# Last down projection, residual and last norm laid out by tokens, in a two-block fp32 transformer kernel

## Chip, core and metric

One NeuronCore of a Trainium2 chip runs the whole program once. The metric is the device time of one execution in microseconds. The core's engines are TensorE (PE in the profile), VectorE (DVE), ScalarE (ACT), GpSimd (POOL) and SyncE (SP, which here only issues DMAs); they run their own instruction streams side by side and meet through semaphores.

## What is computed

256 tokens of width 2048 pass through two blocks, all in fp32. The first block is a hybrid mixer (a state-space part and a gated short convolution), cross attention to a memory and a SwiGLU MLP; the second is an attention layer with three kinds of heads and a gated MLP with a short convolution on its gate. What the change touches is the end:

```python
    # second block; x is [256 tokens, 2048]
    x = x + einsum('bse,ed->bsd', y, w_o)                       # residual after attention
    h = rmsnorm_2(x, ffn_norm)
    g = causal_dwconv_2(h @ w_gate, conv_w, conv_b)
    u = h @ w_up                                                # width 5632
    x = x + (silu(g) * u) @ w_down                              # last down projection
    return rmsnorm_2(x, final_norm)                             # x * rsqrt(mean(x^2) + 1e-6) * final_norm
```

## The kernel before

**Layout.** Activations stand with features on the 128 partitions and tokens along the free axis: the residual `X` is 16 tiles of 128 features x 256 tokens. Every fp32 operand is split into two fp32r numbers, high and low: the weights into `whi` and `wlo`, the activations into the two halves of the buffers `H` and `Y`. A product is high x high + high x low + low x high.

**Weight stream.** All weights come in one fixed order as 930 subs of eight 128x128 blocks (512 KB each). SP loads a sub into one of four `raw` buffers; ACT copies it to `whi` (`split`, L830), DVE subtracts to give `wlo` (`split`, L1227); `whi` and `wlo` are rings of five (`NW`). ACT may only split sub s once PE has finished sub s - 5 (`sub_done`).

**Products.** `gemm_tiles()` lists the tiles in order; `tensor_program` walks them. In the usual form a block of weights is the stationary operand: one matmul of 512 columns (`whi` with the pair of activation halves) and one of 256 (`wlo` with the high half). In the narrow form (`NARROW`, among them `ao2`) it is three of 256. In the wide form (`WIDE`: `wv`, `va`, `vb`, `vc`) the activations of 128 tokens are stationary and `whi` or `wlo` of up to four blocks move: three matmuls for each k and each half t of the tokens, the result lies by tokens. The second MLP's down projection has three parts, `d10`, `d11`, `d12`, of 256, 256 and 192 blocks, in the usual form, eight tiles each. Two accumulators of two PSUM banks alternate between tiles; four further banks serve side work.

**Order.** The stream is cut into slots of four blocks. In the slot where a block count is reached each engine's program runs `side.step(t)` (norms, attention tasks, transposes, each a generator that goes one step per slot), then on odd slots `split(t // 2 + 5)`, then `leave` (takes a finished tile out of its accumulator, on DVE in the tile's last slot plus `GATHER_LAG`, on ACT plus `LAG`) and on DVE `follow` (three slots later). Each engine does this strictly in its own order. So in DVE's program the residual addition of an `ao2` or `d` tile (`leave`, L1675 and L1677) stands behind the split of the same slot. PE runs `side.step` after the last matmul of a slot.

**End.** The last norm (`norm` with n = 6) is summed over features: ACT squares each pair of tiles, POOL adds seven of the eight squares, PE multiplies the sums by a matrix of ones, partly in the stream (before `d12`'s last tile is through), partly after it. Then DVE and ACT make the root with a Newton refinement on 128x256. ACT multiplied each tile by `final_norm_2` before; DVE multiplies six pairs by the root (L1210), POOL two (L1779), and SP and ACT store each pair as it is ready (L471, L1199).

Of the kernel before, what the change touches and what calls it, by code (L numbers as in the profile page):

```python
# [13 lines left out]
P = 128  # L14
# [16 lines left out]
    ("conv_w_2", 132), ("conv_b_2", 44), ("final_norm_2", 16), ("dt_bias", 1), ("a_log", 32),  # L31
# [32 lines left out]
WIDE = ("wv", "va", "vb", "vc")  # L64
NARROW = ("bc", "dt", "xs", "xo", "ao2")

HELD = ("wq", "g0", "qa", "g1", "d00", "d01", "d02", "d10", "d11", "d12")
# [10 lines left out]
def gemm_tiles():  # L78
# [13 lines left out]
    for f in range(2):  # L92
# [6 lines left out]
        for part, (a0, a1) in enumerate(PARTS):  # L99
            for j in range(a0 // 2, a1 // 2):  # L100
                out += [(f"g{f}", j, "H", 0, 16, 2), (f"u{f}", j, "H", 0, 16, 2)]
            out += [(f"d{f}{part}", j, "Y", 0, a1 - a0, 2) for j in range(8)]
# [58 lines left out]
NORM = {"x": 0, "wo2": 1, "xo": 2, "d02": 3, "mid": 4, "ao2": 5, "d12": 6}  # L161
RESIDUAL = ("wo1", "wo2", "xo", "d00", "d01", "d02", "ao1", "ao2", "d10", "d11", "d12")
# [3 lines left out]
def tasks():  # L166
# [21 lines left out]
    out += [(first_slot("g1") + 5, "norm", 5), (N_SLOT - 3, "norm", 6)]  # L188
# [5 lines left out]
LAG = {"bc": 4, "xs": 5, "z": 3, "g0": 1, "g1": 1, "wo2": 2, "xo": 2, "d02": 2, "ao2": 2}  # L194
# [15 lines left out]
for _t, _kind, _i in TASKS:  # L210
# [15 lines left out]
    "xs": [("b", 6, 8, "xs_copy", 1, 1)],  # L226
    "ssd": [("b0", 0, 2, "ssd_exp", 2, 1), ("b1", 0, 2, "ssd_exp", 2, 2), ("o", 6, 9, "ssd_z", 1, 1)],
# [72 lines left out]
def idle(n):  # L300
# [5 lines left out]
    "pe_own act_own dve_own pool_own raw0 raw1 raw2 raw3 x0 x1 x2 x3 x4 x5 x6 x7 c1 raw_first whi_first wlo_first scaled vec mem c2 rel rows hank out "  # L306
# [9 lines left out]
    "bnd_s bnd_max bnd_exp bnd_w bnd_turn bnd_copy bnd_pv bnd_sq bnd_n bnd_root bnd_y gain_x pool_x"  # L316
# [3 lines left out]
class Chip:  # L320


    def __init__(self, nc, ctx, d, out):
# [50 lines left out]
        self.HK = AR[:, 3072:5120]  # L374
        self.rows = nc.dram_tensor("rel_rows", [8, 512], F32).ap()
# [16 lines left out]
    def xt(self, k, n=1):  # L392
        return self.X[:, k * T:(k + n) * T]

# [44 lines left out]
def sync_program(e, c):  # L439
# [29 lines left out]
    for i in range(6):  # L469
        s.wait_ge("gain_x", i + 1)  # L470
        e.dma_start(c.out[:, 2 * i * T:(2 * i + 2) * T], c.xt(2 * i, 2)).then_inc(c.sems["out"], 16)  # L471
    s.wait_ge("out", 128)
# [4 lines left out]
def tensor_program(e, c):  # L477
# [19 lines left out]
    def norm(n):  # L497
# [3 lines left out]
        p.wait_ge("sum_add", 7 * n + (6 if n == 6 else 7))  # L501
        if n < 6:
            last = mm(bank, c.ones, c.SUM, True, True)
        else:
            mm(bank[:, 0:T], c.ones, c.SUM[:, 0:T], True, False)
            mm(bank[:, 0:T], c.ones, c.SUM[:, T:2 * T], False, False)
            yield from idle(3)
            p.wait_ge("sq", 8 * n + 8)
            mm(bank[:, 0:T], c.ones, c.SQ[1][:, 0:T], False, False)
            last = mm(bank[:, 0:T], c.ones, c.SQ[1][:, T:2 * T], False, True)  # L510
        p.then_inc(last, "norm_sum")
# [232 lines left out]

    def done(stage, j):

        b, n = bank_of(stage, j)
        return f"acc{b}", n + 1

    side = Side({"norm": norm, "mnorm": mnorm, "mcol": mcol, "rcol": rcol, "sc": sc, "cb": cb, "dt": dt, "xs": xs, "ssd": ssd,  # L750
                 "grp": grp, "xa": xa, "dfa": dfa, "dfb": dfb, "stk": stk, "bnd": bnd})
# [19 lines left out]
    for stage, j, op, k0, K, m in GEMM:  # L771
# [3 lines left out]
        if stage in WIDE:  # L775
            for k in range(k0, k0 + K):
                wh, wl = halves(b, m)
                for t in range(2):
                    out, start = c.acc[n][:, t, 0:m * P], k == k0
                    xh, xl = c.hi(op, k)[:, t * P:(t + 1) * P], c.lo(op, k)[:, t * P:(t + 1) * P]  # L780
                    mm(out, xh, wh, start, False)
                    mm(out, xl, wh, False, False)
                    last = mm(out, xh, wl, False, k == k0 + K - 1)
                b = finish(b, m, last)
# [14 lines left out]
    for t in range(N_SLOT, N_SLOT + 4):  # L799
        side.step(t)  # L800
# [1115 lines left out]
```

## Time and profile before

| | |
|---|---|
| median of 3 runs | 2743.03 us (2742.43 to 2743.47) |
| the profiled execution | 2743.26 us, of which the span of instructions is 2741.3 us |
| PE busy | 2717.2 us, 99% |
| DVE busy | 1949.9 us, 71% |
| ACT busy | 1284.8 us, 47% |
| POOL busy | 94.7 us, 3% |
| DMA | 499 MB, mean 182 GB/s |
| granted TensorE clock | 0.998 of 2.4 GHz |

All times in the views are microseconds from the start of the span. A matmul is recorded from its start to its modelled end, and matmuls overlap in the array, so what a matmul costs the stream is the distance from its start to the next one's start, not its recorded length.

### The profile page before, as it was taken

The page shows a single profiled execution, that of the slowest core. Times are in us where ns is not written, and L with a number is a line of the kernel's source. Part 1 is how long each engine was busy: PE and PEld are TensorE (multiplying, and loading weights), DVE is VectorE, ACT ScalarE, POOL GpSimd, SP SyncE. Part 2 cuts the span into 40 slices and gives each one's busy share as a digit, 9 for nine tenths or more (in the row PEclk, how much of TensorE's full clock was granted, in tenths as well). Part 3 has the DMA queues.
Part 4 walks back from the last instruction along what each step waited for, and adds up shares of the span by engine and source line. Part 5 has one row for each costly group of instructions (what it writes and reads, how often), then busy time and mean ns, then how long its engine had stood idle before and what let it go on. Part 6 is the DMA issues. An engine that isn't in the chain of part 4 may idle for free.

```text
span 2741.3 us, 39113 instructions
## 1 busy us (share of the span) xinstructions
PE 2717.2 (99%) x16174; PEld 2378.5 (87%) x16174; DVE 1949.9 (71%) x2378; ACT 1284.8 (47%) x1634; POOL 94.7 (3%) x69
## 2 busy tenths in 40 slices
PE   8999999999999999999999999999999999999998
PEld 7888999888898888888888888888988888888886
DVE  7777777876768665666566886776777757775775
ACT  5444455754545443344344554545544433443444
POOL 1000000011101000000000110000100000000001
PEclk9999999999999999999999999999999999999999
DMA  6555555446555555555555555454455555555553
GB/s 240 191 185 185 175 164 173 145 160 223 182 169 189 187 191 194 191 190 189 190 185 193 191 183 170 150 168 144 164 183 185 200 190 178 193 199 190 187 192 124
DMA packets 138192, 499.07 MB, mean 182 GB/s; under 512 B 15248, under 2 KB 16280, under 8 KB 137888
## 3 DMA queue, kind: packets, MB, share of 16 engines
q1 hardware_dynamic: 136224, 491.67, 54.2%
q10 hardware_dynamic: 1792, 4.91, 0.5%
q8 instruction: 127, 2.08, 0.3%
q14 instruction: 49, 0.40, 0.0%
HBM read 494.41 MB, written 2.11 MB: 181 GB/s over the span
## 4 chain that ended last, share of the span: by engine, by line
PE 98%; DVE 1%; DMA 1%; ACT 0%; POOL 0%; issue 0%; DVEq 0%; ACTq 0%; POOLq 0%
PE PS L481 97%; DMA raw<-in_w_in 0%; DVE wlo L1227 0%; POOL AR L1738 0%; ACT whi L830 0%; DMA XG<-in_x 0%; DVE XG L1677 0%; DVE XG L1210 0%; PE PS L573 0%; DVE H L1221 0%; PE PS L727 0%; PE PS L649 0%; ACT AR L837 0%; PE PS L616 0%; DVEq L1785 0%
## 5 line engine op out<-in xcount | busy, mean ns | idle before, releaser
L481 PE MATMUL PS<-H,whi 128*128 128x512 f32 (+1 forms) x5472 | 1788.9, 381 | 8.7 <-DVE wlo L1705 7.9
L1227 DVE TENSOR_TENSOR wlo<-raw,whi 128x1024 fp32r<-128x1024 f32 x929 | 1127.7, 1231 | 638.5 <-ACT whi L830 634.5
L481 PE MATMUL PS<-H,wlo 128*128 128x256 f32 x5072 | 1412.6, 278 | 0.0
L830 ACT ACTIVATE whi<-raw 128x1024 fp32r<-128x1024 f32 x929 | 969.5, 1057 | 921.2 <-PE PS L481 883.2
L481 PEld LDWEIGHTS PS<-H,whi 128*128 128x128 f32 x5472 | 1001.8, 188 | 220.7 <-issue 8.8
L481 PEld LDWEIGHTS PS<-H,wlo 128*128 128x128 f32 x5072 | 956.3, 189 | 3.5 <-issue 3.1
L481 PE MATMUL PS<-Y,whi 128*128 128x512 f32 (+1 forms) x2240 | 719.0, 376 | 1.1 <-DVE XG L1677 0.8
L481 PE MATMUL PS<-Y,wlo 128*128 128x256 f32 x2048 | 569.3, 278 | 0.0
L481 PEld LDWEIGHTS PS<-Y,whi 128*128 128x128 f32 x2240 | 407.8, 188 | 84.0 <-DVE XG L1677 2.0
L481 PEld LDWEIGHTS PS<-Y,wlo 128*128 128x128 f32 x2048 | 385.6, 188 | 0.5 <-issue 0.2
L1549 DVE TENSOR_REDUCE AR<-PS 128x512 f32<-128x1024 f32 x140 | 171.6, 1225 | 14.6
L1738 POOL TENSOR_TENSOR AR<-AR 128x512 f32<-128x512 f32 x48 | 70.5, 1470 | 2003.8 <-ACT AR L837 2002.8
L815 ACT ACTIVATE AR<-AR 128x512 f32<-128x512 f32 x64 | 40.5, 633 | 211.8 <-DVE AR L1237 138.4
L481 PE MATMUL PS<-whi,H 128*128 128x512 f32 (+1 forms) x384 | 105.0, 361 | 0.0
L1210 DVE TENSOR_TENSOR AR<-AR 128x512 f32<-128x512 f32 x114 | 78.9, 692 | 34.7 <-ACT AR L815 32.3
L481 PE MATMUL PS<-AR 128*128 128x256 f32 (+8 forms) x580 | 99.4, 354 | 2.8 <-ACT AR L837 2.2
L1144 ACT ACTIVATE Y<-AR 128x512 fp32r<-128x512 f32 x44 | 27.8, 632 | 150.0 <-DVE AR L1666 150.0
L1237 DVE SCALAR_TENSOR_TENSOR AR<-AR 128x255 f32<-128x255 f32 (+2 forms) x192 | 92.9, 484 | 6.8
L481 PEld LDWEIGHTS PS<-AR 128*128 128x128 f32 (+3 forms) x580 | 61.5, 170 | 22.4 <-issue 11.6
L481 PEld LDWEIGHTS PS<-whi,H 128*128 128x128 f32 x384 | 67.0, 189 | 10.3 <-issue 1.0
L1219 DVE TENSOR_TENSOR Y<-AR,Y 128x512 fp32r<-128x512 f32 (+1 forms) x68 | 42.7, 628 | 37.4 <-ACT Y L1144 34.5
L481 PE MATMUL PS<-wlo,H 128*128 128x512 f32 (+1 forms) x192 | 68.2, 355 | 0.0
(173 smaller groups left out, 895.6 us busy)
## 6 DMA issues: line engine op xcount, KB each, us to landing
raw<-in_ffn SPq DMA_DIRECT2D x528, 512.0 KB, 4.1
raw<-in_w_in SPq DMA_DIRECT2D x177, 512.0 KB, 4.5
raw<-in_w_qkv SPq DMA_DIRECT2D x96, 512.0 KB, 3.7
raw<-in_w_out SPq DMA_DIRECT2D x64, 512.0 KB, 4.2
raw<-in_w_o SPq DMA_DIRECT2D x40, 512.0 KB, 3.6
raw<-in_w_q SPq DMA_DIRECT2D x8, 512.0 KB, 3.9
raw<-in_w_k SPq DMA_DIRECT2D x8, 512.0 KB, 4.3
raw<-in_w_v SPq DMA_DIRECT2D x8, 512.0 KB, 4.6
```

The source lines that it names most:

```text
L481: return e.matmul(out, l, r, start=start, stop=stop)
L815: return e.activation(dst, src, ACT.Silu)
L830: a.then_inc(e.activation(c.whi[:, s % NW, :], c.raw[:, s % NRAW, :], ACT.Copy), "whi")
L1144: a.then_inc(e.activation(c.hi("Y", 2 * (j - 8 * part), 2), two(q), ACT.Copy), "y_hi")
L1210: return e.tensor_tensor(two(dst), two(src), both(r), ALU.mult)
L1219: v.then_inc(e.tensor_tensor(c.lo(op, k, n), src, hi, ALU.subtract), made_)
L1227: v.then_inc(e.tensor_tensor(c.wlo[:, s % NW, :], c.raw[:, s % NRAW, :], c.whi[:, s % NW, :].bitcast(F32), ALU.subtract), "wlo")
L1237: v.then_inc(e.scalar_tensor_tensor(dst[:, sh:T], src[:, 0:T - sh], taps(width - 1 - sh), dst[:, sh:T], ALU.mult, ALU.add), name if sh == ...
L1549: v.then_inc(e.tensor_reduce(two(dst), c.acc[b].rearrange("p m (h t) -> p m t h", h=2), AX, ALU.add), f"acc{b}", turn + 1)
L1738: g.then_inc(e.tensor_tensor(c.SUM, c.SUM, c.SQ[i % 2], ALU.add), "sum_add")
```

## The change

The down projection of the second MLP, parts `d10`, `d11` and `d12`, goes over to the wide form: four tiles of four blocks' width in each part, with the weights as moving operand and the result by tokens. The residual is turned for it: eight side tasks `xt`, one for each `ao2` tile, transpose two tiles of `X` on PE (four transposes of 128x128) in the second slot after the tile's end, once DVE's residual addition of that tile is done; ACT copies the bank to `XT`. The last norm's gain is loaded as a 1 MB tensor repeated over the partitions. `XT` is [128 tokens, 2 halves, 2048]; DVE adds each accumulator of 128x1024 to it.

In `d12` the last tile is walked in two orders: for its first four k both token halves together, for its last eight first half 0 and then half 1. A semaphore `half` marks half 0's last matmul. The norm is now a sum along the free axis: ACT's square with an accumulated sum for each piece of 512 features and each half. For pieces 0 to 2 the squares are made in the stream, and DVE multiplies them by the gain. At the end each half runs its own chain: addition, square, sum, mean, root, Newton on one column; then DVE finishes pieces 3 and 2, which SP stores, and ACT pieces 0 and 1, which it stores as 512 KB in one. POOL no longer takes part in the last norm, and PE no longer has the norm's matmuls. The host lays the weights out in the new order and reads the output by tokens.

```diff
-WIDE = ("wv", "va", "vb", "vc")
+WIDE = ("wv", "va", "vb", "vc", "d10", "d11", "d12")
-HELD = ("wq", "g0", "qa", "g1", "d00", "d01", "d02", "d10", "d11", "d12")
+HELD = ("wq", "g0", "qa", "g1", "d00", "d01", "d02")
+LAST = ("d12", 3)
...
-            out += [(f"d{f}{part}", j, "Y", 0, a1 - a0, 2) for j in range(8)]
+            out += [(f"d{f}{part}", j, "Y", 0, a1 - a0, 4 if f else 2) for j in range(4 if f else 8)]
...
+    out += [(END[NUM["ao2", j]] // 4 + 1, "xt", j) for j in range(8)]
-    out += [(first_slot("g1") + 5, "norm", 5), (N_SLOT - 3, "norm", 6)]
+    out += [(first_slot("g1") + 5, "norm", 5)]
...
@@ sync_program
-    for i in range(6):
-        s.wait_ge("gain_x", i + 1)
-        e.dma_start(c.out[:, 2 * i * T:(2 * i + 2) * T], c.xt(2 * i, 2)).then_inc(c.sems["out"], 16)
+    for t in range(2):
+        for n, j in enumerate((3, 2)):
+            s.wait_ge("gain_x", 2 * t + n + 1)
+            e.dma_start(c.out[:, c.tok(t, j)], c.XT[:, c.tok(t, j)]).then_inc(c.sems["out"], 16)
@@ tensor_program
+    def xt(j):
+        bank = take("xt", j, "b")
+        p.wait_ge(*done("ao2", j))
+        for t in range(2):
+            for i in range(2):
+                last = e.transpose(bank[:, t * T + i * P:t * T + (i + 1) * P], c.xt(2 * j + i)[:, t * P:(t + 1) * P], c.ident)
+        p.then_inc(last, "xt_turn")
+        yield
...
         if stage in WIDE:
...
+            begin, both_halves = b, K - 8 if (stage, j) == LAST else K
+            order = [(k, t) for k in range(both_halves) for t in range(2)]
+            order += [(k, t) for t in range(2) for k in range(both_halves, K)]
+            for k, t in order:
+                if version:
+                    p.wait_ge("y_made", made(version, k))
+                wh, wl = halves(begin + k * m, m)
+                out, start = c.acc[n][:, t, 0:m * P], k == 0
+                xh, xl = c.hi(op, k)[:, t * P:(t + 1) * P], c.lo(op, k)[:, t * P:(t + 1) * P]
+                mm(out, xh, wh, start, False)
+                mm(out, xl, wh, False, False)
+                last = mm(out, xh, wl, False, k == K - 1)
+                if t:
+                    b = finish(begin + k * m, m, last)
+                elif (stage, j) == LAST and k == K - 1:
+                    p.then_inc(last, "half")
@@ scalar_program
+    def xt(j):
+        if j == 0:
+            a.wait_ge("y_made", made("ao", 15))
+            e.dma_start(c.fgain, c.d["fgain"]).then_inc(c.sems["fgain"], 16)
+        yield
+        a.wait_ge("xt_turn", j + 1)
+        dst = c.XT.rearrange("p (t n) -> p t n", t=2)[:, :, j * T:(j + 1) * T]
+        a.then_inc(e.activation(dst, c.bank("xt", j, "b").rearrange("p (t n) -> p t n", t=2), ACT.Copy), "xt_copy")
+        yield
...
+        if stage == "d12" and j < 3:
+            a.wait_ge(*done(stage, j))
+            for t in range(2):
+                final_square(j, t)
+            load(LN_EXP)
...
+    for t in range(2):
+        a.wait_ge("last_x", t + 1)
+        final_square(3, t)
+        r = c.fst[:, 10 + t:11 + t]
+        refine(r, c.fst[:, 8 + t:9 + t], "fin_mean", t + 1, "fin_root")
+        a.wait_ge("fin_gain", 6)
+        a.wait_ge("fin_ok", t + 1)
+        for j in range(2):
+            a.then_inc(e.activation(c.XT[:, c.tok(t, j)], c.XT[:, c.tok(t, j)], ACT.Copy, scale=r))
+        a.wait_ge(*a.at)
+        e.dma_start(c.out[:, c.tok(t, 0, 2)], c.XT[:, c.tok(t, 0, 2)]).then_inc(c.sems["out"], 16)
@@ vector_program, leave and follow
+        if stage in ("d10", "d11", "d12"):
+            b, turn = bank_of(stage, j)
+            x = c.XT.rearrange("p (t n) -> p t n", t=2)[:, :, j * 512:(j + 1) * 512]
+            v.wait_ge("xt_copy", 2 * j + 2)
+            v.wait_ge("sub_done", subs(stage, j))
+            v.wait_ge(*v.at)
+            v.then_inc(e.tensor_tensor(x, x, c.acc[b], ALU.add), f"acc{b}", turn + 1)
...
+        if stage == "d12" and j < 3:
+            v.wait_ge("fgain", 16)
+            v.wait_ge("fsq", 2 * j + 2)
+            for t in range(2):
+                x = c.XT[:, c.tok(t, j)]
+                v.then_inc(e.tensor_tensor(x, x, c.fgain[:, j * 512:(j + 1) * 512], ALU.mult), "fin_gain")
@@ vector_program, end
+    b, _ = bank_of(*LAST)
+    for t in range(2):
+        x2, x3 = c.XT[:, c.tok(t, 2)], c.XT[:, c.tok(t, 3)]
+        m, r, u = (c.fst[:, i + t:i + t + 1] for i in (8, 10, 12))
+        if t:
+            v.wait_ge("sub_done", N_SUB)
+        else:
+            v.wait_ge("half", 1)
+        v.wait_ge(*v.at)
+        v.then_inc(e.tensor_tensor(x3, x3, c.acc[b][:, t, :], ALU.add), "last_x")
+        v.wait_ge("fsq", 7 + t)
+        v.then_inc(e.tensor_reduce(m, c.fst[:, 4 * t:4 * t + 4], AX, ALU.add))
+        v.wait_ge(*v.at)
+        v.then_inc(e.tensor_scalar(m, m, 1.0 / 2048, c.col("eps6"), ALU.mult, ALU.add), "fin_mean")
+        newton(r, m, u, "fin_root", t + 1, "fin_ok")
+        v.wait_ge(*v.at)
+        v.then_inc(e.scalar_tensor_tensor(x3, x3, r, c.fgain[:, 1536:2048], ALU.mult, ALU.mult), "gain_x")
+        v.then_inc(e.tensor_scalar(x2, x2, r, None, ALU.mult), "gain_x")
```

## Rows read from the trace of the kernel before

**Rows 1.** The page's part 1: busy time, share of the span, instructions.
```profile
PE 2717.2 (99%) x16174; PEld 2378.5 (87%) x16174; DVE 1949.9 (71%) x2378; ACT 1284.8 (47%) x1634; POOL 94.7 (3%) x69
```
**Rows 2.** The waits of PE: total, times, longest; four shorter lines follow.
```profile
PE PS L481 <- DVE wlo L1705: 7.9, 1, 7.9
```
**Rows 3.** The chain that ended last, at its end: start, length, what.
```profile
2725.46 0.72 PE PS L481 x4
...
2726.21 0.70 DVE XG L1675
...
2727.65 0.64 ACT AR L837
...
2732.61 0.69 DVE XG L1210
2733.30 1.67 DVEq L1785
```
**Rows 4.** Stores: 40 slices of 0.425 us from 2725; engines' busy and DMA.
```profile
GB/s 0 0 0 0 0 0 0 0 0 0 0 0 0 0 0 0 0 0 0 0 0 140 386 92 260 386 381 207 294 390 371 381 390 386 381 386 106 0 0 0
...
2736.90:2740.40 3.50, 0.00 (x0) 0.00 (x0) 1.54 (x3) 0.00 (x0) 0.00 (x0) 0.50 1.00 372
```
**Rows 5.** Stretches d10, va, vb, ao2: length, PE busy (count), clock, DMA, GB/s.
```profile
2170.42:2259.17 88.75, 88.75 (x514) 1.00 0.61 201
...
1619.50:1663.55 44.05, 44.05 (x198) 1.00 0.60 198
...
1745.52:1773.97 28.45, 28.45 (x140) 1.00 0.43 140
1945.84:1991.90 46.06, 46.06 (x386) 1.00 0.56 183
```
**Rows 6.** Timeline of PE in va, first and last of 12 groups: start, length.
```profile
1639.76 0.62 PE L481 MATMUL PS<-whi,H 128*128 128x512 f32 x2
...
1647.92 0.39 PE L481 MATMUL PS<-whi,H 128*128 128x512 f32 x1
```
**Rows 7.** Timeline of ACT and DVE around an ao2 tile's end.
```profile
1957.61 1.06 ACT L830 ACTIVATE whi<-raw 128x1024 fp32r<-128x1024 f32 x1 [0.50 <-PE PS L481]
1958.71 1.23 DVE L1227 TENSOR_TENSOR wlo<-raw,whi 128x1024 fp32r<-128x1024 f32 x1 [0.86 <-ACT whi L830]
1960.04 0.69 DVE L1677 TENSOR_TENSOR XG<-XG,PS 128x512 f32<-128x512 f32 x1
```
**Rows 8.** Timeline of PE around a group of four transposes, stage xs.
```profile
387.18 0.40 PE L481 MATMUL PS<-H,whi 128*128 128x256 f32 x2
...
387.54 0.60 PE L573 MATMUL PS<-AR 128*128 128x128 f32 x4
...
388.33 0.28 PE L481 MATMUL PS<-H,whi 128*128 128x256 f32 x1
```
**Rows 9.** Timeline of PE in xo, where it waits for DVE's addition.
```profile
819.86 0.50 PE L481 MATMUL PS<-Y,whi 128*128 128x256 f32 x2 [0.39 <-DVE XG L1677]
```
**Rows 10.** Groups by form on ACT and DVE, and DMA issues to landing.
```profile
L982 ACT ACTIVATE AR<-AR 128x2 f32<-128x2 f32 x1 | 0.2, 205 | 1.1 <-DVE AR L1398 1.1
L1413 DVE TENSOR_TENSOR AR<-AR 128x1 f32<-128x1 f32 x1 | 0.2, 159 | 0.0
L1536 DVE TENSOR_SCALAR AR<-AR 128x256 f32<-128x256 f32 x8 | 2.8, 348 | 0.0
raw<-in_ffn SPq DMA_DIRECT2D x528, 512.0 KB, 4.1
AR<-in_mem ACTq DMA_DIRECT2D x1, 2048.0 KB, 10.1
out<-XG SPq DMA_DIRECT2D x6, 256.0 KB, 2.3
```
**Rows 11.** Timeline of PE around the norm's matmuls in d12's last tile.
```profile
2721.98 0.40 PE L481 MATMUL PS<-Y,whi 128*128 128x512 f32 x1
...
2723.54 0.40 PE L481 MATMUL PS<-Y,whi 128*128 128x512 f32 x1
```

## Prediction of the time

> **What bounds the kernel now.** Start with the page's table of engines: PE is busy in 99% of the span [rows 1]. A busy share alone proves no bound, so the waits of PE come next: its one wait for weights, 7.9 us, is for the first of them [rows 2], and the view has four lines besides, 4.1 us together, none for weights. So up to the last down projection the time is PE's own stream, and what DVE, ACT or a DMA does there is worth nothing until PE waits for it. Then the tail, in the chain of waits: PE's last matmul of `d12` ends at 2726.18 us, the span at 2741.3 [rows 3]: 15.1 us. They are two additions of the accumulator, a square, the sum over partitions on PE, mean, root and Newton steps on 128x256, then eight gains of 128x512 and their stores. One gain on DVE takes 0.69 us and the next, beside POOL's own, 1.67 [rows 3]; the last 3.5 us of stores move 372 GB/s at a DMA share of 1.00 [rows 4], so the tail's end is the drain of 2 MB.
>
> **1. Matmul form.** Now each 128x128 block of weights costs a matmul of 512 columns and one of 256. `d10` has 256 blocks and lasts 88.75 us [rows 5], 346.7 ns a block (its 514 matmuls are 512 and one at each border: nothing else is in it). In the wide form the weights move: six matmuls of 512 columns for four blocks and both token halves. The columns stay 768 a block; instructions fall from 2 to 1.5. The trace has this form in `va`: from 1639.76 to 1647.92 us stand 12 groups of three matmuls, 0.680 us each [rows 6]; two groups do four blocks, so 340.0 ns a block. Gain 6.7 ns x 704 blocks (256 + 256 + 192) = 4.7 us. The worse bound: the whole of `va`, side work included, 44.05 us for 128 blocks [rows 5], 344.1 ns, gain 1.8 us. Nothing in the trace shows the form faster than 340.0, which I take, since `d10` to `d12` carry no side work.
> The Trainium skill gives less: "TensorE: Matmul & The Clock Gate", section "Back-to-back issue gap", has a warm matmul cost its columns at 2.4 GHz plus about 2.5 ns, so a block would fall from 325.0 to 323.8 ns and the gain be an estimated 0.9 us. The trace disagrees with it: 346.7 ns a block [rows 5], and 227 ns from one 512-column matmul to the next [rows 6].
>
> Does the new stream starve? A sub of 8 blocks is used up in 2.72 us in place of 2.77; ACT splits it in 1.06 us and DVE in 1.23 [rows 7]. DVE's residual work falls (one addition of 128x1024 where four of 128x512 stood). Where a `d` stage begins, its last two operand tiles are now needed after 14 x 1.36 = 19 us, before after 28 blocks, 9.7 us. The last tile holds four subs at once, as its last eight k are walked for half 0 and then for half 1, and frees none for 8 x 0.68 = 5.4 us; the last sub's buffer comes free 2.7 us into the tile, its splits take 1.06 + 1.23 us, with a slot's other work until about 6 us, and its first use is at 5.44 + 6 x 0.68 = 9.5 us. Cost nothing, cover 3.5 us.
>
> **2. Transposes.** Eight tasks of four transposes, one per `ao2` tile. The `xs` stage has the same group: two blocks of 0.36 us with it between them take 387.18 to 388.33, 1.15 us [rows 8], so 0.43 us a group, 3.5 us in all, on PE's path. Bounds: 0.60 us, the group's recorded length, 4.8 us; downwards the rows leave only their rounding, 0.02 us a group, 3.3 us.
> The Trainium skill ("TensorE: Matmul & The Clock Gate", section "Part 4: PE-mode transpose") gives 275 to 390 ns for one such transpose, by which 32 cost an estimated 8.8 to 12.5 us; the trace has four in a row in 0.60 us [rows 8].
>
> **3. A new wait on PE.** The task sits in the second slot after its tile's last, so PE comes to it 8 blocks after the tile's end, and there waits for DVE's residual addition of that tile. Is that done by then? `ao2` lasts 46.06 us for eight tiles [rows 5], 5.76 a tile and 0.36 a block: the second tile ends at 1957.36 and PE comes at 1960.24. DVE's program, though, has a split ahead of that addition, and the split waits for ACT's, which waits for the buffer that the tile's own last block frees. The rows show it in order: ACT's split at 1957.61 after 0.50 us idle on PE, DVE's split at 1958.71, the addition at 1960.04 for 0.69 us, to 1960.73 [rows 7]. So PE waits 0.5 us, each time. What a restart adds is seen in `xo`, where PE waits for the same line: PE's first two matmuls after it take 0.50 us [rows 9], where a pair takes 0.40 [rows 8]. With 0.05 us of hand-over that is 0.15 more: 0.64 us for each of seven tasks and 0.75 for the eighth, which comes in `g1` after 8 x 0.347 us: 5.2 us. It doesn't melt away: ACT's split is anchored to PE's tile end (it sat idle 0.50 us on PE before it [rows 7]), so a later tile end moves the addition with it. Nor does it repay: behind it on PE wait only its own matmuls. Bounds: the bare 0.49 us gives 3.9, a recorded wait of 0.39 as in [rows 9] 3.1, and a second hand-over and restart of 0.1 us in each 6.0.
> ACT's eight copies of the banks (about 0.63 us each, as its square of 128x512 [rows 3]) fall into its idle 0.50 us [rows 7] and the 1.1 us by which each tile grows: nothing, and without that cover 0.1 us a tile. The 1 MB gain through ACT's queue: nothing, as a load of 2 MB through it landed in 10.1 us [rows 10] and PE never waited for weights [rows 2]; without that cover, 2.7 us (1 MB at 386 GB/s [rows 4]).
>
> **4. The norm's matmuls in the stream go.** With them two blocks take 2721.98 to 2723.54, 1.56 us against 0.69 [rows 11]: 0.9 us.
>
> PE's end moves by -4.7 + 3.5 + 5.2 - 0.9 = +3.1 us: later, to 2729.3 us.
>
> **5. The tail.** E is the end of PE's last matmul; half 0 is ready at E - 5.4. For either half: addition 0.70 and square 0.64 [rows 3]; the read of the square's sum, which no row prices, between nothing and a small ACT instruction's 0.205, taken 0.1; reduction, scale and three Newton steps on a column, 0.16 each; Ln and Exp 0.21 each [rows 10]; and nine hand-overs of 0.02 to 0.04: 3.05 us. Bounds: the same without hand-overs 2.7; each small step at 0.2, 3.4. Then DVE scales piece 3 (0.69, done at 3.8) and piece 2 (a scale of 256 columns is 0.348 [rows 10], so between that and 0.69, taken 0.5; done at 4.3), while ACT scales pieces 0 and 1 (0.63 each) and issues their 512 KB at 4.3. Half 0 has all this done at E - 1.1 and drained by E + 1.7, under PE's last matmuls and half 1's chain: its cover is 1.1 us, and every microsecond beyond is the tail's.
> Drain of half 1: bytes move 0.65 us after an issue (first gain ends 2733.30 [rows 3], first bytes near 2734.0), piece 3 from 4.45 to 5.1, the other 768 KB for 2.05 us at 386 GB/s, to 7.15. From last bytes to the span's end 0.9 us (2740.4 to 2741.3). Tail 8.1 us in place of 15.1: gain 7.0. Bounds: the 512 KB store lands in 2.3 us as one of 256 KB does, and 0.4 for the end of the program: 7.0; in the 4.1 us of a 512 KB weight load: 8.8 [rows 10].
>
> **Sum.** The profiled execution took 2743.26 us, span 2741.3 and 2.0 around it. +3.1 - 7.0 = -3.9: 2739.4 us; the runs' median, 2743.03, lies 0.2 lower: 2739.1 us.
>
> **Rivals.**
> (a) The new wait of part 3 isn't there, or PE comes after the addition: 2739.1 - 5.2 = 2733.9 us. For it: PE waits for this addition nowhere in `ao2` today. Against it: today it asks for it a whole tile later. Chance 0.11.
> (b) The wide form pays nothing on `Y`, 346.7 ns as now: +4.7, 2743.8 us, no change. (By the page's rule of part 1: 3.8 above the forecast.) Against it [rows 6]. Chance 0.07.
> (c) The halves of the tail collide: ACT has two squares, four tiny steps, four scalings and two issues in one queue. It decides where half 0's chain passes 4.3 + 1.1 us; +1 to +2 us, 2741. Chance 0.08.
> (d) The change doesn't do what it says: half 0 isn't stored ahead and 2 MB drain after E: one MB more at 386 GB/s, +2.7 us, 2741.8. Against it: half 0's signal sits on its own last matmul, 5.4 us ahead. Chance 0.03.
> (e) Slower: the wide form is dear outside a quiet stretch. `vb` has it too and took 28.45 us for 64 blocks, 444 ns a block [rows 5]. Were that the form's price, not that of the attention's matmuls among them (140 matmuls where 96 are its own), 704 x 97 ns = 69 us come on top of today's blocks, 2813 us. It decides from 340.0 + 3.9/0.704 = 345.5 ns a block for a loss at all, and from about 353 for one that can be measured. Against it: 340.0 in [rows 6]. Chance 0.04.
>
> **Numbers.** The forecast has 0.67. Its bounds: tail -1.1 to +0.8, wait -2.1 to +0.8, transposes -0.2 to +1.3, wide form up to +2.9; not all at once: 2736.7 to 2742. The range takes in (c), (d) and reaches towards (a): 2735.8 to 2742.2. A measurement can tell 0.2%, 5.5 us, from no change, so the borders are 2737.5 and 2748.5. Faster: (a) and the low end of the forecast, 0.11 + 0.08 = 0.19. Slower: (e) and its like, 0.05. Same 0.76.
>
> **What would show it.** `d10` takes 87.0 us, in groups of 0.68 us. The transposes' line appears eight times, seven in `ao2`; PE waits before each, 0.5 us, released by DVE's addition, and `ao2` grows from 46.06 to about 53.5 us. PE's last matmul ends near 2729.3. Half 0's stores are over before half 1's begin; from PE's end to the span's end 8 us. The forecast falls if PE doesn't wait at the transposes (then it is faster), if a wide block isn't 340 ns, if PE waits for `wlo` in the last tile, or if ACT reaches half 1's square late.

## The result, and the profile after

| | median | runs | lowest to highest |
|---|---|---|---|
| before | 2742.97 us | 16 | 2742.12 to 2743.93 |
| after | 2749.12 us | 16 | 2747.97 to 2763.18 |

The ratio is 1.0033, 95% interval 1.0026 to 1.0041: slower, by 0.3% or 6 us in the median, where 4 us of gain were forecast and the range ended at 2742.2. The runs of after fall into two groups: twelve from 2747.97 to 2749.55, four from 2761.89 to 2763.18. The profiled execution (2762.07 us, span 2760.3) is one of the upper group. The kernel before has one group.

First what the prediction spoke of. The waits of PE in the profile of after (total, times, longest), where [rows 2] had no line for the transposes:

```profile
PE PS L493 <- DVE wlo L1748: 8.1, 1, 8.1
PE PS L753 <- DVE XG L1714: 3.7, 8, 0.5
```

L753 is the transposes' line, L1714 the residual addition: PE waits before each of the eight groups. The timeline of PE around the first one:

```profile
1967.67 0.40 PE L493 MATMUL PS<-Y,whi 128*128 128x256 f32 x2
1967.91 0.28 PE L493 MATMUL PS<-Y,wlo 128*128 128x256 f32 x1
1968.58 0.66 PE L753 MATMUL PS<-AR,XG 128*128 128x128 f32 x4 [0.39 <-DVE XG L1714]
1968.99 0.48 PE L493 MATMUL PS<-Y,whi 128*128 128x256 f32 x2
...
1969.43 0.28 PE L493 MATMUL PS<-Y,whi 128*128 128x256 f32 x1
```

From 1967.67 to 1969.43 stand two blocks and the group: 1.76 us, where two blocks alone take 0.72 [rows 8]. Wait and transposes cost 1.04 us together; 0.43 + 0.64 = 1.07 were forecast.

Now the stages, as in [rows 5] (length, PE busy and count, clock, DMA share, GB/s): `d00`, `ao2`, `d10`, the usual tiles of g1 and u1 from `d10` to `d11`, `d11`, and `d12`.

```profile
1020.48:1110.93 90.45, 90.45 (x513) 1.00 0.58 190
1959.22:2012.80 53.58, 50.40 (x413) 1.00 0.54 178
2195.72:2282.78 87.06, 87.06 (x386) 1.00 0.62 204
2282.78:2463.67 180.89, 180.89 (x1025) 1.00 0.55 181
2463.67:2550.78 87.11, 87.11 (x386) 1.00 0.62 205
2686.45:2751.51 65.06, 65.06 (x289) 1.00 0.47 155
```

`ao2` takes 53.6 us (53.5 forecast), `d10` 87.06 (87.0 forecast). But the first row is a stage that the change doesn't touch: `d00`, in the first block's MLP, takes 90.45 us for 256 blocks. The fourth row is 512 blocks in the form that they had before, in 180.89 us. In the kernel before the same two stretches are:

```profile
1017.78:1106.53 88.75, 88.75 (x514) 1.00 0.59 194
2259.17:2436.66 177.49, 177.49 (x1026) 1.00 0.56 184
```

That is 346.7 ns a block before and 353.3 after, with the same instructions, the same granted clock (1.00), no wait of PE (it is busy in the whole stretch) and the same bytes of DMA (184 GB/s for 177.49 us, 181 for 180.89). The timeline of PE shows the two rhythms. Before, from 2299.74 on:

```profile
2299.74 0.40 PE L481 MATMUL PS<-H,whi 128*128 128x512 f32 x1
...
2300.09 0.39 PE L481 MATMUL PS<-H,whi 128*128 128x512 f32 x1
...
2300.43 0.40 PE L481 MATMUL PS<-H,whi 128*128 128x512 f32 x1
...
2300.78 0.39 PE L481 MATMUL PS<-H,whi 128*128 128x512 f32 x1
```

After:

```profile
2299.91 0.40 PE L493 MATMUL PS<-H,whi 128*128 128x512 f32 x1
...
2300.26 0.40 PE L493 MATMUL PS<-H,whi 128*128 128x512 f32 x1
...
2300.61 0.40 PE L493 MATMUL PS<-H,whi 128*128 128x512 f32 x1
...
2300.97 0.40 PE L493 MATMUL PS<-H,whi 128*128 128x512 f32 x1
```

Three blocks take 1.04 us before and 1.06 after. The one rhythm repeats every two blocks: from one block's start to the next 0.343 and 0.350 us, 0.693 together. The other repeats every three: 0.349, 0.350 and 0.361, 1.060 together. In the profile of after the long rhythm holds, without a break, for 2106 blocks from 848 us on (from the norm in g0's first tile through `d02` to the norm that follows it), for 486 blocks of g1 and u1 before `d10`, and for the 896 blocks after `d10` and `d11`. At 6.65 ns a block that is 14.0 + 3.2 + 6.0 = 23.2 us. Taken off the span of 2760.3 us, 2737.1 remain; the forecast of the span was 2741.3 - 3.9 = 2737.4.

The tail, as [rows 3] for before: the chain from PE's last matmul on.

```profile
2750.95 1.15 PE PS L493 x5
...
2752.11 0.70 DVE AR L1775
...
2752.84 0.73 ACT AR L1129 x2
...
2755.08 1.33 ACT AR L1233 x2
```

and the stores, in 40 slices of 0.425 us from 2745, as [rows 4]:

```profile
GB/s 0 0 0 0 0 0 0 0 0 0 0 0 0 0 92 366 400 395 415 405 386 10 0 0 0 0 0 178 381 390 400 414 386 318 0 0 0 0 0 0
```

PE ends at 2752.09, the span at 2760.3: 8.2 us (8.1 forecast, 15.1 before). Half 0's megabyte is gone before half 1's begins.

### The profile page after: what moved, and what is told of

Read it like the earlier page. It is cut to its first block, busy times and chain, and to the rows that moved or that the text cites. A ratio compares the mean times of both kernels' runs of the same rounds, so it can differ in the third digit from the quotient of the medians.

```text
span 2760.3 us, 38409 instructions
## 1 busy us (share of the span) xinstructions
PE 2737.5 (99%) x15846; PEld 2378.1 (86%) x15846; DVE 1934.6 (70%) x2353; ACT 1284.0 (47%) x1640; POOL 83.6 (3%) x61
## 4 chain that ended last, share of the span: by engine, by line
PE 96%; DVE 2%; ACT 1%; DMA 1%; POOL 0%; issue 0%; DVEq 0%; ACTq 0%; POOLq 0%
PE PS L493 95%; DVE wlo L1263 1%; ACT whi L847 1%; DVE XG L1459 0%; DMA raw<-in_w_in 0%; DVE XG L1714 0%; POOL AR L1793 0%; DMA XG<-in_x 0%; PE PS L753 0%; DVE AR L1579 0%; PE PS L576 0%; DVE H L1257 0%; PE PS L730 0%; PE PS L652 0%; PE PS L619 0%
## 5 line engine op out<-in xcount | busy, mean ns | idle before, releaser
L493 PE MATMUL PS<-Y,whi 128*128 128x512 f32 (+1 forms) x1536 | 480.5, 372 | 1.1 <-DVE XG L1714 0.8
L493 PE MATMUL PS<-Y,wlo 128*128 128x256 f32 x1344 | 378.0, 281 | 0.0
L493 PEld LDWEIGHTS PS<-Y,whi 128*128 128x128 f32 x1536 | 276.4, 189 | 55.6 <-DVE XG L1714 2.0
L493 PEld LDWEIGHTS PS<-Y,wlo 128*128 128x128 f32 x1344 | 254.9, 190 | 0.5 <-issue 0.2
L493 PE MATMUL PS<-whi,Y 128*128 128x512 f32 x704 | 217.0, 390 | 0.0
L493 PEld LDWEIGHTS PS<-whi,Y 128*128 128x128 f32 x704 | 132.0, 188 | 27.2
L493 PE MATMUL PS<-wlo,Y 128*128 128x512 f32 x352 | 137.2, 390 | 0.0
L493 PE MATMUL PS<-AR 128*128 128x256 f32 (+9 forms) x572 | 96.9, 353 | 0.7 <-ACT AR L1137 0.6
L493 PEld LDWEIGHTS PS<-wlo,Y 128*128 128x128 f32 x352 | 66.1, 188 | 13.8
```

Source lines behind the costliest of these rows:

```text
L493: return e.matmul(out, l, r, start=start, stop=stop)
```

## The experiments

Theory A: the wait of part 3 of the prediction. Theory B: the usual form has two steady rhythms, and how a stretch starts decides in which it stays. Against B stood C: something in the whole program makes usual blocks slow. Later came D (the addresses of the norm's operands decide how the stream goes on behind a norm) and E (the address of an unused matmul's operands decides the rhythm behind it). A norm's matmul is one fp32 matmul of 512 columns, with a matrix of ones as its stationary operand and the sums as the moving one. Each kernel below was timed beside the kernel before, whose medians lay from 2742.86 to 2743.05 us. "Short" and "long" stand for 346.7 and 353.3 ns a block. Each kernel has one profile; the rhythms of its other executions are inferred from their times.

**Transposes one slot later.**

```diff
-    out += [(END[NUM["ao2", j]] // 4 + 1, "xt", j) for j in range(8)]
+    out += [(END[NUM["ao2", j]] // 4 + 2, "xt", j) for j in range(8)]
```

> The changed kernel with the transposes one slot (four blocks) later, nothing else. In its profile PE waits 3.7 us before the eight groups of transposes, and ao2 lasts 53.6 us. Theory A (the task comes 0.5 us before DVE's addition is done, and the restart costs 0.15 us more each time): the waits on the transposes' line are gone, ao2 lasts about 48.7 us (46.06 and seven groups of 0.43; the eighth now in g1), time 5.2 us less than the changed kernel. Rival (the longer ao2 is the price of the transposes themselves, or the wait moves with the task): ao2 stays above 52 us. The usual blocks of g1, u1 stay at 353.3 ns by theory B (the rhythm after a wide stage), unless the restart after the transposes was what set it in the first eight tiles.

Measured: 2744.11 us, 10 runs, the lower six from 2742.84 to 2744.14: 5.0 us less than after. Both medians are taken over two groups of times; the same edit made later, at the old addresses, where each kernel has one group, gives 5.0 us as well (2745.06 to 2740.02). The line of L753 is gone from the waits of PE, and `ao2` is down to the transposes' own 3.0 us above [rows 5]:

```profile
1960.72:2009.82 49.10, 49.10 (x413) 1.00 0.58 193
2279.08:2459.97 180.89, 180.89 (x1025) 1.00 0.53 181
```

Theory A holds. The second row is the stretch after `d10`: long, as in after. Four of the ten runs were again some 14 us above the rest.

**Two matmuls swapped after each wide stage.**

```diff
+            elif stage == "g1" and j in (8, 16) and (i, k) == (0, 1):
+                mm(bank[:, T:2 * T], wl, c.hi(op, k0 + k), False, False)
+                last = mm(bank, wh, c.pair(op, k0 + k), False, False)
```

> The changed kernel; in g1's tiles 8 and 16, the first after a wide stage, the second block runs its matmul of 256 columns first and its matmul of 512 second. Nothing else: 2 of 15,000 pairs swapped. Theory B (the usual form has two steady rhythms, 346.7 and 353.3 ns a block, and how a stretch starts decides in which it stays; after a wide stage it starts in the slow one): the swap is a new start, and the 512 blocks after d10 and the 384 after d11 may fall into 346.7 ns, 3.4 and 2.6 us less; if the swap's start leads to the slow rhythm as well, nothing changes. Rival C (something about the whole program, such as the shifted addresses or the 1 MB gain, makes usual blocks slow): 353.3 ns whatever is done at the start.

Measured: 2749.26 us (ten runs from 2745.24 to 2763.54), the stretch after `d10` 180.88 us: nothing changed there. Two runs, at 2745.2 and 2746.1, lie some 3 us under the rest of the lower group, as if g1's first stretch had been short in them; no profile shows it. This start leads to the long rhythm too; the run tells nothing between B and C.

**An unused fp32 matmul after each wide stage.**

```diff
+        if stage == "g1" and j in (8, 16):
+            p.wait_ge("norm_mean", 6)
+            mm(c.misc[BANK["norm", 5, "b"][0]], c.ones, c.SUM, True, True)
```

> The changed kernel; before g1's tiles 8 and 16 PE runs one fp32 matmul of 512 columns on data that nobody uses (ones times the old sums), of the kind that stands ahead of the fast stretch of g1 in the kernel before. It costs about 0.85 us at each place. Theory B: the 512 and 384 blocks after it run at 346.7 ns in place of 353.3 if this start leads to the fast rhythm: 6.0 us gained for 1.7 spent, about 4 us less than the changed kernel. Rival C: 353.3 ns, and the time is 1.7 us more.

Measured: 2744.75 us, 4.4 less than after. The stretch after `d10` is short:

```profile
2267.29:2445.19 177.90, 177.90 (x1026) 1.00 0.54 184
```

C falls: the program is the same but for one instruction ahead of the stretch, and 512 blocks follow it in the other rhythm. The ten runs lie in groups: 2741.4 to 2741.6, 2744.1 to 2745.5, 2754.7, and 2759.0 to 2759.2. The profiled one, 2741.59, has every long stretch in the short rhythm. The steps between groups fit the 3.2 us of g1's first stretch and the 14.0 us of g0's, each by itself.

**The long rhythm put into the kernel before.**

```diff
+        if stage == "g1" and j in (8, 16):
+            p.wait_ge("norm_mean", 6)
+            for k in range(3):
+                mm(c.misc[BANK["norm", 5, "b"][0]], c.hi("H", 15)[:, 0:P], c.pair("H", k), True, True)
```

> The kernel before; ahead of g1's tiles 8 and 16 PE runs three fp32r matmuls of 512 columns on data nobody uses (the last group of a wide stage in shape and distance). They cost 3 x 0.227 = 0.7 us at each place, 1.4 us in all. Theory B: they start the usual stream as a wide stage does, and the blocks from tile 8 on run at 353.3 ns instead of 346.7 for as long as nothing disturbs them: at least 512 + 384 blocks, up to all 1344 blocks to the norm's matmuls: 6 to 9 us more on top of the 1.4. Rival C: blocks stay at 346.7 ns, and the time is 1.4 us more.

Measured: 2749.60 us, 6.6 more than before. The stretches of its profile from tile 8 to `d11`, `d11`, and 122 us from tile 16 on:

```profile
2259.89:2440.79 180.90, 180.90 (x1026) 1.00 0.54 181
2440.79:2531.95 91.16, 91.16 (x517) 1.00 0.58 197
2531.95:2653.98 122.03, 122.03 (x706) 1.00 0.55 186
```

Three matmuls of the wide form's shape turn 763 blocks long (to the end of `d11`, in the usual form here): 5.1 us, and 1.4 for the matmuls themselves, in a kernel that has neither transposes nor wide `d` stages. The same three ahead of tile 16, met in the long rhythm, turned it short again: 347 ns in the last row (122.03 us less the three matmuls' 0.7, for some 350 blocks). So the form alone doesn't make what follows long; the rhythm in which it is met seems to count too, seen here once each way.

**A start at four places, with the transposes one slot later.**

```diff
+        if (stage, j) in (("g0", 0), ("g1", 0), ("g1", 8), ("g1", 16)):
...
+            w = 128 if j else 512
+            mm(c.misc[bank][:, 0:w], c.ones, c.c1[:, 0:w], True, True)
```

> The changed kernel with the transposes one slot later and, in addition, one unused fp32 matmul ahead of four stretches: 512 columns before the first tile of g0 and of g1, 128 columns before g1's tiles 8 and 16. The fp32 matmul of 512 columns ahead of tiles 8 and 16 brought 346.7 ns a block there; the first stretches of g0 and g1 were left to themselves and ran now at 346.7, now at 353.3. Theory B: a start after such a matmul leads to the fast rhythm whatever came before, and once fast a stretch stays fast through its transposes and its norm: all usual blocks of both MLPs at 346.7 ns, in all runs, 2738 us (the all-fast run of the kernel with two such matmuls, 2741.5, less 5.1 for the later slot, plus 1.7 and less 1.2 for the sizes). If 128 columns aren't enough to change the rhythm, up to 6 us more, 2744. Rival (what decides is chance at each norm, not the start before it): two or three groups of times 3 and 14 us apart as so far.

Measured: 2742.60 us; ten runs from 2741.25 to 2743.07, two at 2755.5 and 2755.8. In the profile g1's first stretch is short and the 896 blocks after the wide stages are long (180.98 us after `d10`). Of g0's first stretch two runs of twelve are still long. "Whatever came before" was too much: 128 columns changed nothing, and in the profiled execution, an upper one, the blocks behind the 512-column matmul ahead of g0 were long already before g0's norm and stayed so after it.

**The old addresses.** The change took `final_norm_2`, 16 columns, out of the vector table, and everything behind it in that buffer (the ones and the identity, the sums, the small statistics) moved down by 64 bytes. Here the 16 columns are put back, unused.

```diff
-    ("conv_w_2", 132), ("conv_b_2", 44), ("dt_bias", 1), ("a_log", 32),
+    ("conv_w_2", 132), ("conv_b_2", 44), ("final_norm_2", 16), ("dt_bias", 1), ("a_log", 32),
```

> The changed kernel with the old gain kept as 16 unused columns in the vector table, so that all small tiles lie at the addresses they have in the kernel before (the change had moved them by 64 bytes). In the kernel before the first MLP ran at 346.7 ns a block in all of its runs, in the changed one a part of the runs take 13 to 14 us more there, although its program is the same up to that point. Theory D (the addresses decide how the first MLP's stretch starts): no run in the upper group (2758 and above). Theory B alone (chance at each start, from small shifts of time between the engines): about a third of the runs stays in the upper group. Usual blocks after the wide stages stay at 353.3 ns under both.

Measured: 2745.06 us, eleven runs from 2744.65 to 2745.55. One group. `d00` and the stretch after `d10`:

```profile
1017.90:1106.65 88.75, 88.75 (x514) 1.00 0.60 192
2266.33:2447.22 180.89, 180.89 (x1026) 1.00 0.55 181
```

D holds: 16 unused columns take 4.1 us off the median of after, and the spread with it; the waits, loads and semaphores of the change are all still there. g0's and g1's first stretches are short, those after the wide stages long.

**The new addresses in the kernel before.**

```diff
-    ("conv_w_2", 132), ("conv_b_2", 44), ("final_norm_2", 16), ("dt_bias", 1), ("a_log", 32),
+    ("conv_w_2", 132), ("conv_b_2", 44), ("dt_bias", 1), ("a_log", 32),
...
+        self.fnorm = sb("fnorm", [P, 16])[:, 0:16]
```

> The kernel before, its last gain (16 columns) taken out of the vector table into a tile of its own with its own small load, so that everything behind it in that buffer (the ones, the sums, the small statistics) lies 64 bytes lower, as the change has it. Nothing else. Theory D (the address of the norm's operands decides how the stream starts again after a norm): some of its runs have the first MLP at 353.3 ns a block and lie near 2757 us, some the first eight tiles of the second (and all up to the norm at the end: 2076 blocks, up to 14 us more), where the kernel before has 2743 us in all of its runs. Rival (the change's other parts, its waits, loads and semaphores, made the first MLP slow in a part of the runs): all runs at 2743 us.

Measured: 2756.93 us, five runs from 2755.62 to 2757.40, ratio 1.0050 (1.0037 to 1.0062). The 64 bytes of shift cost the kernel before 14 us. The gain's own load of 16 columns, its semaphore and ACT's wait for it in `d12` came with the edit, but in its profile the rhythm turned in g1, over 600 us ahead of that wait, and the run before this one took the loss away by addresses alone. `d00`, the stretch after `d10`, and `d11`:

```profile
1017.40:1106.15 88.75, 88.75 (x514) 1.00 0.59 193
2263.49:2444.39 180.90, 180.90 (x1026) 1.00 0.55 181
2444.39:2534.85 90.46, 90.46 (x514) 1.00 0.61 198
```

It is g1's start, after its norm, that goes long here and holds through 2076 blocks (13.8 us), while g0's is short. The other four runs took as long; whether g1's stretch or g0's (14.0 us) was long in them, their times can't tell, but never both.

**The norm's own matmul, in all profiles.** The timelines of the fifteen kernels with a profile hold more cases of D than these two. An fp32 matmul of 512 columns with the ones as its stationary operand stands in many places of the usual stream (in the norms, and in side tasks of the first block). The table counts those across which the block starts lie 0.80 to 0.82 us apart, with the long rhythm ahead of them. In `qa`'s norm they lie 0.86 to 0.98 apart; it isn't counted, and both rhythms follow it at both addresses.

| address of the ones | the last distance between block starts ahead of it | blocks behind it |
|---|---|---|
| old | any of the three | short in 28 of 28 |
| new | the 0.361, or the second one after it | long in 16 of 16 |
| new | the first one after the 0.361 | short in 8 of 8 |

Where the stream was short ahead of it, it stayed short behind it, 68 of 68 times at the old address and 59 of 60 at the new; the one exception is g0's norm in the profile of after. In the kernel before, the blocks of g1 ahead of its norm are long and the norm turns the stream short; in after, and in the kernel before with the new addresses, they are long too and the norm leaves it so. The matmul's numbers are the same at both addresses.

**All three edits.** Old addresses, later slot, and the unused matmul of 512 columns.

> The changed kernel with three edits put together: the small tiles at their old addresses (the kernel that had this alone ran at 2745.1 us in all its runs, within 0.5), the transposes one slot later (5.1 us less in the pair of profiles and of medians), and an unused fp32 matmul of 512 columns ahead of g1's tiles 8 and 16 (346.7 ns a block after it: 896 blocks, 6.0 us less for 1.7 more). If the three causes are what they seem and add up: 2745.1 - 5.1 - 4.3 = 2735.7 us in all runs, ratio to the kernel before 0.9973. If the starts of the stretches hang on the timing of the engines rather than on addresses, the later slot will have moved it, and some runs lie 3 or 14 us above.

Measured: 2741.71 us, eleven runs from 2741.34 to 2742.12. 6.0 us above the expectation, and the profile says where: the unused matmul has the old addresses now, and the stretches after it are long.

```profile
2261.23:2442.53 181.30, 181.30 (x1026) 1.00 0.55 180
```

The same instruction at the same place brought the short rhythm with the ones and sums 64 bytes lower (and the transposes one slot earlier). The variant with 256 columns:

> As the kernel with all three edits, but the unused fp32 matmul has 256 columns in place of 512. 512 columns changed the rhythm, 128 didn't. If 256 do: 0.2 to 0.4 us less at each place, 2735.2 us. If they don't: the blocks after the wide stages stay at 353.3 ns, 6.0 us more, 2741.0 us.

Measured: 2740.90 us, long as well. It only shows that the smaller one is 0.8 us cheaper.

**Whose address?** Old addresses for all, but the unused matmul reads its stationary operand 64 bytes below the ones, and its moving one 192 bytes above the sums: modulo 256 bytes, where both lay when it brought the short rhythm.

```diff
+            g = 12288 + NVEC
+            w, x = g + 256, g + NC1 + 512
+            dw, dx = (16, -48) if j == 8 else (16, -48)
+            mm(c.misc[BANK["norm", 5, "b"][0]], c.AR[:, w - dw:w - dw + P], c.AR[:, x - dx:x - dx + 512], True, True)
```

> As the kernel with all three edits that took 2741.7 us (old addresses, later slot, unused fp32 matmul of 512 columns ahead of g1's tiles 8 and 16), but that matmul reads its stationary operand 64 bytes below the ones and its moving operand 192 bytes above the sums, so that both addresses have, modulo 256 bytes, the residue that they had in the kernel where this matmul brought the fast rhythm; with the old addresses it had brought the slow one. Theory E (the address of the fp32 matmul's operands decides the rhythm of the stretch after it): 346.7 ns after both, 2741.7 - 6.0 = 2735.7 us, ratio 0.9974. Rival (the address of something else, or the timing, decides): 353.3 ns, 2741.7 us.

Measured: 2735.67 us, eight runs from 2735.39 to 2736.08, ratio 0.9974 (0.9963 to 0.9984). The three edits now add up to what was expected (2735.7), and the kernel is faster than the kernel before and than after. Theory E holds. One operand at a time (`(16, 0)` ahead of tile 8, `(0, -48)` ahead of tile 16):

> As the kernel before this one in the list, but with only one operand of the unused matmul moved at each place: the stationary one ahead of tile 8, the moving one ahead of tile 16. The profile tells which operand's address counts: 346.7 ns from tile 8 on and 353.3 from tile 16 on for the stationary one, the reverse for the moving one, 353.3 in both if both must be moved or neither counts. No difference is expected elsewhere.

Measured: 2738.49 us in one execution. The stretches after tile 8 and after tile 16:

```profile
2261.39:2439.29 177.90, 177.90 (x1025) 1.00 0.55 184
2526.84:2662.92 136.08, 136.08 (x769) 1.00 0.53 179
```

Short after tile 8, 177.9 us for 512 blocks and the matmul; long after tile 16, 136.1 us for 384 blocks where the kernel with both moved takes 133.5. The stationary operand is the one that counts. With its address its numbers changed as well, since 16 of its 128 columns are no longer ones, and no run here parts the two; the norm's matmul, in the table above, has its numbers unchanged.

**The two edits that need no extra matmul.**

> The changed kernel with two edits: old addresses of the small tiles, transposes one slot later. No extra matmuls. The kernel with old addresses alone took 2745.1 us in every run, and the later slot gave 5.1 us. Expected: 2740.0 us, ratio 0.9989, all runs within 1 us; usual blocks at 346.7 ns in g0 and in g1's first eight tiles, at 353.3 after the two wide stages. Rival (old addresses hold the rhythm only for one timing of the engines): runs in groups 3 or 14 us above.

Measured: 2740.02 us, eleven runs from 2739.62 to 2740.16, ratio 0.9989 (0.9980 to 0.9998).

**Half 0 not ahead.**

```diff
-            begin, both_halves = b, K - 8 if (stage, j) == LAST else K
+            begin, both_halves = b, K
```

> The changed kernel with the last tile of d12 walked in one order, both token halves together for all twelve k, so that half 0 is ready only three matmuls (0.7 us) before half 1. The rest is as in the changed kernel. Theory (the halves' chains run one after the other in DVE's and ACT's programs, 4.4 us each up to the last gain, and only the early half 0 hides one of them): from PE's last matmul to the end of the span 11.8 us where the changed kernel has 8.2, 3.6 us more. Rival (the end is bound by the drain of the stores): 2 MB after PE's end at 390 GB/s in place of 1 MB, 2.7 us more. No difference in the rest.

Measured, in the profile: PE's last matmul ends at 2739.34, the span at 2751.1, 11.7 us where after has 8.2: 3.5 us, which is the theory's 3.6 and not the rival's 2.7. The last matmul, and DVE's order in the timeline:

```profile
2738.95 0.39 PE L493 MATMUL PS<-wlo,Y 128*128 128x512 f32 x1
...
2738.70 0.69 DVE L1775 TENSOR_TENSOR AR<-AR,PS 128x512 f32<-128x512 f32 x1 [9.24 <-PE PS L493]
...
2742.33 0.48 DVE L1783 TENSOR_SCALAR AR<-AR 128x512 f32<-128x512 f32 x1
2742.92 0.69 DVE L1775 TENSOR_TENSOR AR<-AR,PS 128x512 f32<-128x512 f32 x1
```

Half 1's addition starts at 2742.92, right behind half 0's last product; its sum had been ready for 3.6 us. The median (2765.39 us, four runs from 2752.91 to 2766.71) isn't compared: by their times three of the four have g0 in the long rhythm.

## Why the prediction missed

**Part 1, matmul form: right, its neighbours missed.** `d10` takes 87.06 us (87.0). The step that failed is the sum: it adds +3.1 - 7.0 to today's span and so puts the change of all stretches outside its five parts at nothing, without a reason. The runs showed 9.2 us there, and 23.2 in those of the upper group. The first part of it is the form's: the 896 usual blocks after `d10` and `d11` start from a wide stage and fall into the long rhythm, 6.0 us, more than the form's own gain of 4.7. The hint stood in the trace of before: its `ka` stage follows the wide `va`, and its first 47 blocks take 353.0 ns each, in the same steps of 349, 350 and 361 ns, before attention's tasks break in. The rule of the Trainium skill that part 1 sets against its rows ("TensorE: Matmul & The Clock Gate", section "Back-to-back issue gap") is given there for a matmul by itself, not for a stream with a weight load ahead of each; here neither rhythm follows it, 346.7 and 353.3 ns against 325.0.

**The missing term, addresses.** The second part of what the sum put at nothing: 16 columns leave the vector table. It costs 3.2 us in g1's first stretch, and in part of the runs 14.0 in g0's. By their times 20 of 62 runs have g0 long over the six changed kernels with the change's addresses, and 0 of 52 over the six with the old ones.

**Parts 2 and 3, transposes and the wait: right.** 1.04 us a group against 1.07; the later slot gave back 5.0 of the 5.2 us charged. Rival (a) falls. The trace records a transpose of 128x128 with 273 ns (the median of the 32). The Trainium skill gives about 275 for one of bf16 in a kernel ("TensorE: Matmul & The Clock Gate", section "Part 4: PE-mode transpose"). That is no price for four in a row: 3.0 us for seven groups in the kernel with the later slot, 0.11 us for each transpose. A slip of the sum: 8 x 0.43 is 3.4, not 3.5.

**Part 4, the norm's matmuls: right within what can be read.** From the start of `d12`'s first matmul to that of its last, the 288th, are 65.06 us: 226.7 ns each, 340.0 ns a block, with nothing of the norm between them. A kernel that differs in these matmuls alone was not run.

**Part 5, the tail: right.** 8.2 us against 8.1; from PE's end to the last Newton step 2.97 us, where the prediction wrote 3.05 and its own terms add up to 2.8 to 3.0. The halves don't collide: DVE was idle for 1.3 us and ACT for 1.8 before half 1. (c) and (d) fall.

**Rivals (b) and (e).** The wide form itself is never dear, so both fall as told. But the loss has (e)'s sign and, in part, a related cause: not the wide block costs more, but the usual one behind it.

**The sum with the missing term.** Old addresses: 2739.1 + 6.0 = 2745.1 us; measured 2745.06. With the change's addresses 3.2 more, 2748.3 (the lower group, 2748.0 to 2749.6), or 3.2 + 14.0 more, 2762.3 (the upper one, 2761.9 to 2763.2).

What stays open: why an address acts. The runs show that the stationary operand of the fp32 matmul at which a stretch starts counts, not by which path it does, and the one-operand test is one execution. Why g0 differs from run to run at the new addresses is answered in part by the table above: the rhythm and the step of it in which the stream meets g0's norm differ between the profiles, and six of the seven with these addresses follow the table; what shifts that step from run to run isn't shown. Nor is it shown why a wide stage starts the long rhythm, nor what else moved by those 64 bytes and may count beside the ones.

## What to carry to other kernels

Where PE is the bound, read the distance between matmul starts in stretches that the change doesn't touch, before and after; a block's price here was a property of a rhythm, not of an instruction, and a profile of 99% busy and full clock hid 2% of it. A change that shifts a buffer's layout is a change of its own: keep old addresses by padding while you judge the rest, and take several runs, since two groups of times are the sign. A side task that sits two slots after its input isn't safe because two slots have passed: read where in the other engine's program the producer stands.

## What the runs showed of the hardware

The same pair of matmuls (512 and 256 columns with a weight load each) settles into one of two steady rhythms, 0.693 us for two blocks or 1.060 for three, at the same granted clock, and keeps it for thousands of matmuls, up to 2106 blocks in these profiles. A short disturbance sets it: three matmuls of 512 columns (0.7 us) turned 763 blocks from one to the other. Which one comes depends on the rhythm before and the step of it that is met (the table above), on the shape of the disturbance (an fp32 matmul of 512 columns brought the short rhythm after a wide stage at one address, one of 128 columns at that address didn't) and on where its stationary operand lies, 64 bytes being enough: 14 us in the kernel before. At the end of after each half's megabyte, two stores of 256 KB and one of 512 KB on two queues, drained at 366 to 415 GB/s while it flowed in full; a store of 256 KB landed 2.2 us after its issue and one of 512 KB 3.4.
